# Forget-gate logits inside the sparse attention's projection, and the forgetting attention run head by head under its chunks

## The reference

```
xn = rms(x, norm_attn)
fq, fk, fv, f_logit, nq, kc, vc, ksl, vsl, kw, vw, nsa_gate, ... = split(xn @ w_in)
#  1024 1024 1024   8      |------------ 3480 columns ------------|
fq = rms(fq per head of 128) * gain;  fk likewise
log_f = log_sigmoid(f_logit + bias)          # 8 heads
c     = cumsum(log_f over tokens)
s     = fq.fk / sqrt(128) + c[query] - c[key], causal
o_a   = softmax(s) @ fv                      # the forgetting attention, 8 heads of 128
o_b   = sparse attention on nq .. nsa_gate   # compressed, selected and window branches
```

## Time and profile before

| | us |
|---|---|
| median of 3 runs | 2925.17 |
| lowest and highest | 2923.25 and 2926.93 |
| the profiled execution's own time | 2920.28 |
| span of its trace, first to last instruction | 2918.5 |
| PE busy in the span | 2697.2 (92%) |
| DVE, ACT busy | 1662.3 (57%), 1199.6 (41%) |
| mean granted clock of PE | 0.967 |

### The profile page before, as it was taken

How to read it: one execution, slowest core, us unless ns; L and a number is a source line. 1 busy time by engine, 2 the same in 40 slices (tenths; PEclk the granted TensorE clock), 3 DMA queues, 4 the chain that set the end, 5 groups by cost and what they waited for, 6 DMA issues and landing times.

```text
span 2918.5 us, 31866 instructions
## 1 busy us (share of the span) xinstructions
PE 2697.2 (92%) x12319; PEld 2227.5 (76%) x12319; DVE 1662.3 (57%) x1843; ACT 1199.6 (41%) x1583; POOL 5.9 (0%) x60
## 2 busy tenths in 40 slices
PE   1499678999999999999989989999999999999999
PEld 0388555778878888888878875888888888888887
DVE  6767767767645555556544555555455545445454
ACT  1244334444433444444434543444444444344343
POOL 0000000000000000000000000000000000000000
PEclk9999789989999999999979978999999999999999
DMA  8777356768655555555425540555555565555654
GB/s 339 292 278 277 141 201 214 254 210 284 223 181 189 188 187 194 196 187 188 144 85 191 176 143 1 188 185 190 194 181 186 188 196 191 189 194 180 201 187 144
DMA packets 256911, 566.01 MB, mean 194 GB/s; under 512 B 12069, under 2 KB 27170, under 8 KB 244258
## 3 DMA queue, kind: packets, MB, share of 16 engines
q1 hardware_dynamic: 254272, 562.86, 56.5%
q10 hardware_dynamic: 2530, 1.65, 0.2%
HBM read 562.38 MB, written 2.10 MB: 193 GB/s over the span
## 4 chain that ended last, share of the span: by engine, by line
PE 87%; DVE 9%; ACT 1%; issue 1%; ACTq 1%; DMA 1%; DVEq 0%; PEldq 0%
PE acc L416 80%; DVE acc_ada L1336 3%; PE tp L430 2%; DVE w_lo L369 1%; PE acc L2587 1%; PE tp L2256 1%; PE acc L2658 0%; DMA perow<-in_cmp_pe_v_dram 0%; ACT w_hi L364 0%; PE acc L2657 0%; DVE mxs L1583 0%; ACTq L627 0%; DVE mxs L1884 0%; PE sc L2670 0%; PE sc L2642 0%
## 5 line engine op out<-in xcount | busy, mean ns | idle before, releaser
L369 DVE TENSOR_TENSOR w_lo<-w_raw,w_hi 128x1024 fp32r<-128x1024 f32 (+1 forms) x890 | 1055.2, 1208 | 615.7 <-ACT w_hi L364 609.8
L364 ACT ACTIVATE w_hi<-w_raw 128x1024 fp32r<-128x1024 f32 (+1 forms) x890 | 916.0, 1047 | 916.2 <-PE acc L416 868.0
L416 PE MATMUL acc<-w_hi,h_hi 128*128 128x512 f32 (+2 forms) x2304 | 713.6, 391 | 21.7 <-DVE h_lo L1407 11.2
L416 PE MATMUL acc<-w_lo,h_hi 128*128 128x512 f32 (+2 forms) x2304 | 708.5, 389 | 0.0
L416 PE MATMUL acc<-w_hi,h_lo 128*128 128x512 f32 (+2 forms) x2304 | 707.9, 388 | 0.0
L416 PEld LDWEIGHTS acc<-w_hi,h_hi 128*128 128x128 f32 x2304 | 430.9, 190 | 108.3 <-issue 12.8
L416 PEld LDWEIGHTS acc<-w_hi,h_lo 128*128 128x128 f32 x2304 | 436.4, 190 | 87.7
L416 PEld LDWEIGHTS acc<-w_lo,h_hi 128*128 128x128 f32 x2304 | 435.9, 190 | 87.6
L416 PE MATMUL acc<-w_hi,f_hi 128*128 128x512 f32 x864 | 269.2, 393 | 5.3 <-DVE w_lo L369 4.7
L416 PE MATMUL acc<-w_hi,f_lo 128*128 128x512 f32 x864 | 267.3, 391 | 0.0
L416 PE MATMUL acc<-w_lo,f_hi 128*128 128x512 f32 x864 | 267.2, 390 | 0.0
(11 more groups left out here) (388 smaller groups left out, 1750.2 us busy)
## 6 DMA issues: line engine op xcount, KB each, us to landing
w_raw<-in_w_ff_dram SPq DMA_DIRECT2D x128, 1024.0 KB, 5.1
w_raw<-in_w_in_dram SPq DMA_DIRECT2D x108, 1024.0 KB, 5.0
w_raw<-in_w_ada_dram SPq DMA_DIRECT2D x96, 1024.0 KB, 4.9
w_raw<-in_w_ffn_gate_dram SPq DMA_DIRECT2D x44, 1024.0 KB, 5.1
w_raw<-in_w_ffn_up_dram SPq DMA_DIRECT2D x44, 1024.0 KB, 5.0
w_raw<-in_w_ffn_down_dram SPq DMA_DIRECT2D x44, 1024.0 KB, 5.0
w_raw<-in_w_out_dram SPq DMA_DIRECT2D x32, 1024.0 KB, 5.0
w_raw<-in_w_up_fox_dram SPq DMA_DIRECT2D x8, 1024.0 KB, 5.0
```

Of the source, the lines that this page charges most:

```text
L364: nc.scalar.activation(dst, src, ACT.Copy).then_inc(hi_done, 1)
L369: nc.vector.tensor_tensor(dst, src, hi.bitcast(F32), ALU.subtract).then_inc(lo_done, 1)
L416: last = nc.tensor.matmul(acc[b][:, t, 0:width], st[:, kt, t * P:(t + 1) * P], w[:, slot, kt - 2 * j, 0:width], start=(kt == 0 and n == 0) ...
```

## The change

The projection of fq, fk and fv keeps its six chunks and loses the chunk of 8 columns. The second projection starts 8 columns earlier, at the logits: seven chunks, six full and one of 416 columns, into a tile `wide` whose first 8 columns are the logits and whose other 3480 are `nsa`. The last drain of the first projection (`leave_last=True`) and the second four groups of transposes (`turn_late`) move under chunk 0 of the second projection. The log-sigmoid, cumulative sum and the eight heads are cut into pieces that each engine runs after given halves: piece g belongs to chunk 1 + g/8. `fox_unit(g, lag)` says which head has its turn: head u starts at g = 5 + 4u with its scores, its maxima lie at g+3 (DVE), Exp at g+4 (ACT), scaling at g+5 (DVE), transposes at g+3 (PE), `pfT` at g+6 (ACT), values at g+5 (PE), `oT` at g+8 (DVE). These are each engine's own counts of halves. Scores go to `sc[0]` and values to `sc[1]`, since `acc` is in use. The tiles move to other places in SBUF, `heads_squared` does nine heads and writes its unread squares to SBUF, and three heads are squared in the stage behind. The heads' operations and their shapes stay as they were. The second projection is written out chunk by chunk (`uniform=0`) where it had a loop that ran once.

```
+FOX_FIRST, FOX_STEP = 5, 4
...
+        wide = place("logits_and_nsa", [P, NT, HEADS + NSA_W], F32, 56.75)
+        nsa = wide[:, :, HEADS:HEADS + NSA_W]
...
+        def fox_unit(g, lag):
+            u, rest = divmod(g - FOX_FIRST - lag, FOX_STEP)
+            return u if rest == 0 and 0 <= u < HEADS else None
...
 # SP
-            weights(w2, 7, KD, uniform=6, widths={6: HEADS})
-            weights(w2, 7, KD, col0=NSA0, uniform=6, widths={6: NSA_W - 6 * CW})
+            weights(w2, 6, KD)
+            weights(w2, 7, KD, col0=F_LOGIT0, uniform=6, widths={6: HEADS + NSA_W - 6 * CW})
...
 # PE
-            weights(7, KD, h_hi, h_lo, uniform=4, widths={6: HEADS},
-                    first=turned_x("x_gained", use),
-                    during={5: turn_early, 6: turn_late})
-            pe.wait_ge(S("logf_made"), 1)
...
-            causal("fox", HEADS, pf, pfT, fox_scores, fox_values)
-            pe.wait_ge(S("fox_o"), HEADS)
+            weights(6, KD, h_hi, h_lo, uniform=4, first=turned_x("x_gained", use), during={5: turn_early})
...
+            def fox_part(g):
+                if g == 3:
+                    pe.wait_ge(S("logf_made"), 1)
+...
+                u = fox_unit(g, 0)
+                if u is not None:
+                    if u == 0:
+                        pe.wait_ge(S("ctok_made"), 1)
+                    else:
+                        pe.wait_ge(S("fox_max"), u)
+                    fox_scores(u, sc[0]).then_inc(S("fox_scores"), 1)
+                u = fox_unit(g, 3)
+                if u is not None:
+                    pe.wait_ge(S("fox_probs"), u + 1)
+                    TR(pe, At(probs_use + u), [((slice(0, P), slice(k * P, (k + 1) * P)), pf[u % 2][:, k * P:(k + 1) * P])
                                               for k in range(3)])
+                    pe.sem_inc(S("fox_turned"), 1)
+                u = fox_unit(g, 5)
+                if u is not None:
+                    pe.wait_ge(tp_free[at.slot(2)], at.round(2).val(1))
+                    if u >= 1:
+                        pe.wait_ge(S("fox_o"), u)
+                    fox_values(u, pfT[u % 2]).then_inc(S("fox_pv"), 1)
...
+            weights(7, KD, h_hi, h_lo, uniform=0, widths={6: HEADS + NSA_W - 6 * CW},
+                    during={0: turn_late, **{c: during_nsa(c) for c in range(1, 7)}})
...
 # DVE: log_gates(g) at g = 2, 4, 6, then per head
+                u = fox_unit(g, 3)      # wait fox_scores; bias, mask, maxima
+                u = fox_unit(g, 5)      # wait fox_exp; reciprocal, scaling
+                u = fox_unit(g, 8)      # wait fox_pv; copy to oT
...
 # ACT: Exp and Ln of the gates at g = 3, then per head
+                u = fox_unit(g, 4)      # wait fox_max; Exp with sums
+                u = fox_unit(g, 6)      # wait for the transposes; copy to pfT
...
-                        squares([(t, head) for head in (10, 11) for t in range(NT)])
+                        for heads in ((9, 10), (11,)):
+                            squares([(t, head) for head in heads for t in range(NT)],
+                                    [sc[b % 2][:, b // 2 * QH:(b // 2 + 1) * QH] for b in range(4)])
```

More of the change, by code:

```diff
@@ L220, in build @@
         gfin = [place(f"gfin{c}", [P, CW], F32, kib) for c, kib in enumerate((64, 66, 72, 82))]
[L222 to L229, removed]
@@ L239, in build @@
[L239 to L244, removed]
+        fox = place("fox", [P, NT, 3 * FOX_W], F32, 16)
+        foxsq = place("foxsq", [P, NT, 2 * FOX_W], F32, 57)
+        fqT = place("fqT", [P, HEADS, T], F32, 40)
+        fkT = place("fkT", [P, HEADS, T], F32, 48)
@@ new lines, in build @@
+        pf = [place(f"pf{b}", [P, CAUSAL], F32, 16 + 1.5 * b) for b in range(2)]
+        pfT = [place(f"pfT{b}", [P, CAUSAL], F32, 19 + 1.5 * b) for b in range(2)]
+        unread = place("unread", [P, 4, QH], F32, 28)
+        flog = place("flog", [P, NT, HEADS], F32, 56)
+        logf = place("logf", [P, 4, NT * HEADS], F32, 56.25)
+        ctok = place("ctok", [P, NT, HEADS], F32, 56.5)
+        wide = place("logits_and_nsa", [P, NT, HEADS + NSA_W], F32, 56.75)
+        nsa = wide[:, :, HEADS:HEADS + NSA_W]
@@ new lines, in build @@
+        kp = [place(f"kp{n}", [P, CMP * ROWS + 98], F32R, 16 + 4.25 * n) for n in range(4)]
+        kp_f = [place(f"kpf{n}", [P, CMP * ROWS], F32, 33 + 3.75 * n) for n in range(2)]
+        kcr = place("kcr", [P, GROUPS, T], F32, 40.5)
+        kcr6 = place("kcr6", [64, GROUPS, T], F32, 42.5)
+        vcr = place("vcr", [P, GROUPS, T], F32, 44.5)
+        peT = place("peT", [P, 3, CMP], F32, 46.5)
+        hid = place("hid", [ROWS, 2, HID], F32, 47)
+        hidT = place("hidT", [P, 2, 2, ROWS], F32, 49)
@@ L245, in build @@
+        kcn = place("kcn", [ROWS, 2, QH], F32, 50)
+        kcT = place("kcT", [P, ROWS], F32, 54.5)
+        kcT6 = place("kcT6", [64, ROWS], F32, 54.75)
+        vc = place("vc", [NB, GROUPS, P], F32, 55)
         w2k = place("w2k", [P, 2, QH], F32, 84)
@@ L992, in fox_drain @@
             def fox_drain(c):
[L993 to L1010, removed]
+                if c.known() and c.k == 0:
+                    act.wait_ge(S("mix2_rstd"), 1)
@@ new lines, in fox_drain @@
+                fox_out(c)
+            weights(6, KD, fox_drain, uniform=4, during={4: square_part, 5: during_v}, first=first_fox, leave_last=True)
+            use += 16
+            probs_use = use
+            def fox_part(g):
+                if g == 3:
+                    act.wait_ge(S("flog_abs"), 1)
+                    link(nc.scalar.activation(logf[:, 2, :], logf[:, 1, :], ACT.Exp, scale=-1.0))
+                    nc.scalar.activation(logf[:, 3, :], logf[:, 2, :], ACT.Ln, bias=1.0).then_inc(S("flog_ln"), 1)
+                u = fox_unit(g, 4)
+                if u is not None:
+                    act.wait_ge(S("fox_max"), u + 1)
+                    for t, (lo, hi) in enumerate(((0, P), (P, CAUSAL))):
+                        k = 24 + 2 * u + t
+                        last = nc.scalar.activation(pf[u % 2][:, lo:hi], pf[u % 2][:, lo:hi], ACT.Exp,
+                                                    bias=mxs[:, k:k + 1], accum_out=sums[:, k:k + 1])
+                    last.then_inc(S("fox_exp"), 1)
+                u = fox_unit(g, 6)
+                if u is not None:
+                    bank, free = tp_wait(act, At(probs_use + u))
+                    if u >= 2:
+                        act.wait_ge(S("fox_pv"), u - 1)
+                    nc.scalar.activation(pfT[u % 2][:], bank[:, 0:CAUSAL], ACT.Copy).then_inc(free, 1)
@@ L1029, in causal, with squares @@
                 use += units
-            causal("fox", HEADS, pf, pfT, 0)
             nsa_acc = n.acc
-            def squares(todo):
+            def squares(todo, places):
                 for n_th, (t, head) in enumerate(todo):
-                    unread = sc[n_th % 2][:, n_th // 2 * QH:(n_th // 2 + 1) * QH]
                     col = head * QH + (0, KS0 - 8 * QH, KW0 - 10 * QH)[(head >= 8) + (head >= 10)]
                     k = 12 * t + head
-                    last = nc.scalar.activation(unread, nsa[:, t, col:col + QH], ACT.Square,
+                    last = nc.scalar.activation(places[n_th], nsa[:, t, col:col + QH], ACT.Square,
                                                 accum_out=sums[:, k:k + 1])
                 link(last)
-            early_heads = [(t, head) for head in range(10) for t in range(NT)]
+            early_heads = [(t, head) for head in range(9) for t in range(NT)]
             def heads_squared(j):
@@ L1052, in heads_squared @@
                         act.wait_ge(acc_free[a % 2], 2 * (a // 2) + 2)
-                    squares(early_heads[4 * (j - 2):4 * (j - 1)])
+                    squares(early_heads[4 * (j - 2):4 * (j - 1)], [unread[:, b, :] for b in range(4)])
                     if j == 6:
@@ L1069, in raw_keys, with during_nsa, after @@
                     nc.scalar.activation(dst[:].rearrange("p a b -> p (a b)"), bank[:], ACT.Copy).then_inc(free, 1)
-            nsa_out = copy_out(nsa, KD, {6: NSA_W - 6 * CW}, rstd=stat[:, 14:15])
-            weights(7, KD, nsa_out, uniform=4, widths={6: NSA_W - 6 * CW}, leave_last=True,
-                    during={5: heads_squared, 6: raw_keys})
+            w6 = {6: HEADS + NSA_W - 6 * CW}
+            nsa_out = copy_out(wide, KD, w6, rstd=stat[:, 14:15])
+            def during_nsa(c):
+                def after(j):
+                    fox_part(8 * (c - 1) + j)
+                    if c == 5:
+                        heads_squared(j)
+                    elif c == 6:
+                        raw_keys(j)
+                return after
+            use += 8
+            weights(7, KD, nsa_out, uniform=0, widths=w6, leave_last=True,
+                    first=lambda j: fox_out(At(5)) if j == 1 else None,
+                    during={0: during_logits, **{c: during_nsa(c) for c in range(1, 7)}})
             use += 4
@@ L1830, in during_logits @@
                     fox_turned(3 + j)
```

(43 more changed lines are left out.)

125 lines of the change are left out of this document (60 added, 65 removed).

## The result

The changed kernel takes 2901.66 us (median of 4 runs, 2895.82 to 2907.34), the kernel before 2926.05 (4 runs, 2923.25 to 2927.82). The ratio is 0.992, interval 0.9901 to 0.9939. Timed again beside the experiments it gave 2901.79 (6 runs) and 0.9918, interval 0.9903 to 0.9933. So 24 us are won, where 33.7 were forecast; the time lies inside the stated range, 10 above the point, and in the part of the range that belongs to rival B.

What follows compares the result with a forecast made beforehand. PE was taken as the bound, busy 92% of the span; 59.3 removed less 24.8 back on PE less 0.85 for squares gave 33.7 us less, 2886.6 profiled, 2891.5 against the median; range 2882 to 2908.

Steps and rivals of the forecast that it cites:

- rival B: Heads under the second projection: waits come due before the chains are through; 2897 to 2918 us, chance 0.11.
- What was removed: Stretch dissolved before the full chunks, 59.3 us: narrow chunk 20.4, gates and cumulative sum 5.7, heads 32.0, DVE's first subtraction 1.3.
- The price of PE's work: Back on PE between full chunks, 24.8 us: transpose groups 2.0, cumulative sum 0.7, eight heads 21.8, eight more columns 0.3.
- rival D: Small float32 matmuls and transposes let the clock fall in the new place; heads up to 41 us, 2911; chance 0.03.
- So I cost the hand-overs at nothing: Heads' waits between PE, ACT and DVE hidden under three or four halves of PE: 0 us, slack 2.4 for probabilities.
- A: As forecast, 2886 to 2897 us, chance 0.76.
- The table load: ACT's gates: 1.28 us a load by the rows; the skill's rule adds about 1.38 drain, stalling PE about 1.3 once.
- The squares: Compression stage: six squares in ACT's order where four stood, 0.85 us not hidden, bounds 0 and 1.5.
- Rival C: Slower: strict order starves the ring at 24 hand-overs on PE; 54 us comes back, 2946; chance 0.03.
- Rival E: More won: compression starts with another phase of the clock, or breaks cost nothing; 2880 to 2886 us, chance 0.07.

Runs made afterwards that it cites:

- FOX_FIRST 7: Changed kernel with the constant at 7 in place of 5, every piece of every head two halves later: 2888.66 us, ratio 0.9882, stretch 184.56.

## Why the prediction was right or wrong

**What was removed.** 59.3 us, as put together from four parts. No 8-column matmul is left on the line of the products, and `ctok` and the gates cost PE nothing: the wait for `logf` does not show. Right. With 23.1 forecast and 23.2 found for the narrow chunk and the gates, this part is right in size too.

**The price of PE's work** was right to 0.05 in every term. With FOX_FIRST 7, which has no waits, the stretch is 184.56, and the forecast's terms give 219.7 - 34.5 = 185.2. The transposes 0.33 for 0.38, scores 1.55, values 0.65; the clock 1.00 throughout. This also answers rival D: in this kernel, transposes and small float32 matmuls among full chunks left the clock at 1.00 for 140 us. The rule that spoke for the rival (the Trainium skill, page "TensorE: Matmul & The Clock Gate", section "Part 4: PE-mode transpose"), that transposes do not count as PE activity for the full clock, has nothing to show for it here, with 39 transposes in those 140 us, 24 of them the heads'. But at 0.11 each they fill only about 4 us, so that this is a weak test of how transposes count, and the prediction's "does not bear it out" was stronger than its rows.

**The step that failed** is "So I cost the hand-overs at nothing". Its count of what the probabilities must pass had two splits and the softmax, ready 7.3 after the end of half g0 and asked for at 9.7. For head 0 the trace has them asked for at 9.8 and ready at 12.95 (1506.67 to 1519.62). It left out what the clockwork itself does behind half 1 of each chunk: ACT's drain, which waits for PE's end of the previous chunk. For heads 0, 2, 4 and 6 the Exp stands right behind it. For head 2 the profile has PE's end at 1545.84 and the scaled tile at 1550.30, 4.5 later, and PE asks one half after the end of the chunk: 2.8 later. Hence 1.8 of stall, three times, and 3.2 the first time, where 1.28 of table load is added. What the four cost in the stretch, 195.65 - 184.56 = 11.1, is accounted for: 8.6 of waits, 4.34 - 2.78 = 1.6 of slow clock behind the longest, and 4 x (0.55 - 0.33) = 0.9 of the transposes that start from standstill. The cause was tried in three ways, by the order on ACT (6.5 won), by the place of the heads (11.0) and by the place of the drain (9.6), so it is shown and not only argued. Rival B was the one that named such a thing, with a price of 2.3 a head for eight heads; it was 2.8 for four. So what came is rival B, which had 0.11, and not A, which had 0.76 and ended at 2897. That the measured 2901.66 lies in the range is owed to the nearer half of B in it: the range held, the mechanism forecast for the hand-overs did not.

**The table load** was weighed by a rule (the Trainium skill, page "ScalarE: Activation LUTs", section "What ACT_TABLE_LOAD costs") and set aside by the rows. The rows of after bear that out for the gates: the second load starts 1.53 after the first, so that the drain of about 1.38 that the section adds to each load does not show, `logf` is ready 8.2 after the end of chunk 0 where 9.4 was forecast, and PE does not wait for it. But the load counted at another place than the one that I looked at, before the heads' first Exp, the third of the three loads, and there it is 1.4 of wait and 1.6 of clock.

**The squares** in the compression stage: 0.85 forecast. The first stall there is 1.3 us against 0.42 before, so the size is right where it arises; that the squares are its cause follows from their place in ACT's order, and no run tested it. Whether it arrives at the end the whole times can't tell, as the stage scatters by more.

**Rival C**, a starved ring: not seen. `lo_done` is not among PE's waits under the second projection. **Rival E** gave a few microseconds to the clock of the stage behind. In ten profiles the stage took 151.6 to 166.2, which is wider than that, and eight of the nine others lie above the 152.7 of the kernel before: where the clock moved the stage, it mostly made it longer. The sum left it as it was, and in the first profile of the changed kernel it nearly stayed so (151.6).

## What to carry to other kernels

When work is laid under a clockwork whose engines keep strict order, list first what the clockwork itself waits for at each place, and put no link of a chain at, or right behind, such a wait; here moving eight heads by two halves, one constant, won 11 us of the 35 that were there. Ask of each link not only whether its engine has time but what it must pass: a wait on ACT also held the next `w_hi`, the `w_lo` made from it, and DVE's step behind that. When a forecast for a stretch and its measurement differ, compare the same stretch between fixed instructions: in two profiles of one kernel it agreed to 0.1 us, while whole times scattered by 10. And subtract the part itself (here the heads) from both kernels: a gain of 24 us hid that the overlap had won less than 1.

## What was not expected of the hardware

One stall of PE cost more than itself: after 3.2 us without work the granted clock was 0.65 in the next 4.84 us, a mean of its two levels, and 12 matmuls took 4.34 where others take 2.78; after stalls of 1.8 us the same 12 took 2.77. Windows of the stall, of what followed, and of the next 5 us (columns as before):

```profile
1516.43:1519.66 3.23, 0.00 (x1) 0.00 (x1) 1.90 (x5) 2.21 (x4) 0.00 (x0) 1.00 0.00 0
1519.66:1524.50 4.84, 4.84 (x17) 3.89 (x18) 2.30 (x2) 1.43 (x2) 0.00 (x0) 0.65 0.52 154
1524.50:1529.50 5.00, 5.00 (x30) 4.37 (x29) 2.48 (x5) 2.57 (x6) 0.00 (x0) 1.00 0.16 61
```

Three transposes took 0.55 from standstill, after the stalls of 1.8 us too, and 0.33 in the stream. And the stage with many short waits took 151.6 to 166.2 us with the same work in it (only the kernel before has two squares less there), its sparse attention at a granted clock of 0.81 in one profile and 0.71 in another.
